# The beginning of a transformer kernel: loads on two queues, item 0 and x in three pieces, squares and a weight split shared out

## What is computed

```python
def _rmsnorm(x, g):
    r = lax.rsqrt(jnp.mean(x * x, axis=-1, keepdims=True) + EPS)
    return x * r * g

def _swiglu(x, w_gate, w_up, w_down):            # 1024 -> 2816 -> 1024
    return (silu(x @ w_gate) * (x @ w_up)) @ w_down

# ffn1:  x + 0.5 * rmsnorm(_swiglu(_rmsnorm(x, pre_g), ...), post_g)
```

## Time and profile before

| | |
|---|---|
| median of three runs | 1083.72 us |
| the profiled execution | 1082.73 us |
| its span, first to last instruction | 1080.9 us |
| TensorE matmuls, busy | 1065.5 us (99%) |
| VectorE busy | 794.4 us (73%) |
| ScalarE busy | 592.9 us (55%) |
| GpSimd busy | 218.5 us (20%) |
| moved by DMA | 189.64 MB |

### The profile page before, as it was taken

One profiled execution on the slowest core, in us unless ns is written; L12 is line 12 of the kernel. 1 busy time (PEld: TensorE's weight loads), 2 busy tenths in 40 slices (PEclk: granted clock), 3 DMA queues, 4 the chain that ended last, 5 costly groups with the idle time before them and its releaser, 6 DMA issues.

```text
span 1080.9 us, 18754 instructions
## 1 busy us (share of the span) xinstructions
PE 1065.5 (99%) x7012; PEld 937.8 (87%) x7012; DVE 794.4 (73%) x1096; ACT 592.9 (55%) x857; POOL 218.5 (20%) x225
## 2 busy tenths in 40 slices
PE   9999999999999999999999999999999999999997
PEld 8888889888788888898997988888899888888886
DVE  5867776897678888766795788777559557777674
ACT  6546544767766445455796644544433565544453
POOL 0006000031069997000000497000000000000001
PEclk9999999999999999999999999999999999999999
DMA  7765455342445556552434655645434235545541
GB/s 260 294 246 200 182 177 199 132 154 79 145 167 186 216 179 229 181 208 98 142 134 157 251 190 178 233 175 181 169 133 161 97 121 188 221 175 184 207 152 39
DMA packets 37025, 189.64 MB, mean 175 GB/s; under 512 B 3824, under 2 KB 4592, under 8 KB 22640
## 3 DMA queue, kind: packets, MB, share of 16 engines
q1 hardware_dynamic: 34528, 181.22, 46.5%
q10 hardware_dynamic: 2160, 6.70, 1.8%
q0 software_dynamic: 288, 1.05, 0.3%
HBM read 187.90 MB, written 1.05 MB: 175 GB/s over the span
## 4 chain that ended last, share of the span: by engine, by line
PE 88%; DVE 6%; ACT 4%; issue 1%; DMA 1%; SPq 0%; DVEq 0%; ACTq 0%
PE ps L567 23%; PE ps L638 19%; PE ps L572 12%; PE ps L679 7%; PE ps L803 6%; PE ps L579 6%; PE ps L599 2%; DVE gu_low L1833 1%; PE ps L701 1%; PE ps L527 1%; PE ps L614 1%; PE ps L755 1%; PE ps L626 1%; PE ps L786 1%; PE ps L768 1%
## 5 line engine op out<-in xcount | busy, mean ns | idle before, releaser
L567 PE MATMUL ps<-hT,gu_high 128*128 128x512 f32 x1152 | 286.7, 391 | 0.0
L567 PEld LDWEIGHTS ps<-hT,gu_high 128*128 128x128 f32 x1152 | 211.5, 188 | 41.5 <-DVE gu_low L1968 0.4
L1968 DVE TENSOR_TENSOR gu_low<-gu_raw,gu_high 128x2048 fp32r<-128x2048 f32 x83 | 196.3, 2366 | 7.6 <-ACT gu_high L1307 4.6
L572 PEld LDWEIGHTS ps<-hT,gu_low 128*128 128x128 f32 x1152 | 157.2, 190 | 11.2
L1307 ACT ACTIVATE gu_high<-gu_raw 128x2048 fp32r<-128x2048 f32 x84 | 160.4, 1909 | 9.3 <-PE ps L579 8.2
L572 PE MATMUL ps<-hT,gu_low 128*128 128x256 f32 x1152 | 160.6, 282 | 0.0
L1283 ACT ACTIVATE ffn_s<-ffn_s 128x256 f32<-128x256 f32 x88 | 36.8, 418 | 181.3 <-DVE ffn_s L1935 145.4
L1972 DVE TENSOR_TENSOR dn_low<-dn_raw,dn_high 128x1024 fp32r<-128x1024 f32 x84 | 112.2, 1336 | 2.7 <-ACT dn_high L1315 2.7
L1950 DVE TENSOR_TENSOR ffn_s<-ps,ffn_s 128x256 f32<-128x256 f32 x72 | 30.6, 425 | 108.4 <-ACT ffn_s L1295 108.4
L1315 ACT ACTIVATE dn_high<-dn_raw 128x1024 fp32r<-128x1024 f32 x84 | 88.7, 1056 | 35.6 <-PE ps L638 35.6
L1182 ACT ACTIVATE gu_high<-gu_raw 128x2048 fp32r<-128x2048 f32 x37 | 70.8, 1914 | 67.5 <-PE ps L679 36.6
(11 more groups left out here) (337 smaller groups left out, 1874.3 us busy)
## 6 DMA issues: line engine op xcount, KB each, us to landing
gu_raw<-in_wgu SPq DMA_DIRECT2D x126, 1024.0 KB, 4.8
dn_raw<-in_wdn SPq DMA_DIRECT2D x88, 512.0 KB, 5.4
x<-in_x SPq DMA_DIRECT2D x2, 512.0 KB, 5.4
gu_raw<-in_wgu SPq DMA_DIRECT2D x2, 512.0 KB, 6.5
scratch<-in_glu ACTq DMA_DIRECT2D x1, 1024.0 KB, 7.5
scratch<-in_biasM ACTq DMA_DIRECT2D x1, 1024.0 KB, 5.0
s5in<-in_s5in ACTq DMA_DIRECT2D x1, 768.0 KB, 4.4
out_x<-scratch SPq DMA_DIRECT2D x3, 256.0 KB, 2.4
```

The source lines that it names most:

```text
L567: nc.tensor.matmul(out, gu[0][:, sl, o:o + P], hT_both[:, k, :, :].rearrange("p a s -> p (a s)"), start=k == 0, stop=False)
L572: i = nc.tensor.matmul(out[:, 0:SEQ], gu[1][:, sl, o:o + P], hT[0][:, k, :], start=False, stop=k == KC - 1)
L1968: nc.vector.tensor_tensor(gu[1][:, sl, :], gu_raw[:, sl, :], gu[0][:, sl, :], ALU.subtract).then_inc(s["gu_split"], 1)
```

## The change

Loads:
- x goes to ScalarE's queue, in three pieces: columns 0 to 255, 256 to 511, 512 to 1023; `cols` is issued after the first. Item 0 stays on SyncE's queue, in three pieces of the same columns (for gate and up together). Item 1 is loaded in two halves with a semaphore each. dn 0 and dn 1 now come ahead of the loop over guarded loads.

TensorE: chunks are transposed in pairs (both tiles of chunks 2k and 2k + 1) by `first_transposes(k)`: pairs 0 and 1 before the first matmul, pair 2 before k = 2, pair 3 before k = 4. The seven fillers are gone.

ScalarE: each quarter of item 0 waits for its own piece. Then: item 1's first half, the square of tile 0, item 1's second half, both roots, dn 0.

VectorE: the square of tile 1 by a `tensor_tensor_reduce` between item 1's two remainders. dn 0's remainder moves to GpSimd, and VectorE waits for it before it adds its own first count to `dn_split`.

```diff
-            for h, arrived in enumerate(("first_loaded", "gu_loaded0")):
-                hs = slice(h * 512, h * 512 + 512)
-                sp_.dma_start(x[:, :, hs], a["x"][:, :, hs]).then_inc(s["x_loaded%d" % h], 16)
-                sp_.dma_start(by_gate(gu_raw)[:, :, hs], first_item[:, :, hs]).then_inc(s[arrived], 16)
+            for arrived, ks in (("first_loaded0", slice(0, 256)), ("first_loaded1", slice(256, 512)),
+                                ("gu_loaded0", slice(512, 1024))):
+                sp_.dma_start(by_gate(gu_raw)[:, :, ks], first_item[:, :, ks]).then_inc(s[arrived], 16)
+            for w, arrived in enumerate(("second_loaded", "gu_loaded1")):
+                ws = slice(w * 1024, w * 1024 + 1024)
+                sp_.dma_start(gu_raw[:, 1, ws], a["wgu"][1][:, ws]).then_inc(s[arrived], 16)
...
-            for g in range(1, 4):
-                if g == 2:
-                    for d in range(2):
-                        load_dn(d, d, guard=False)
-                load_gu(g, g % 2, guard=g >= 2)
+            for d in range(2):
+                load_dn(d, d, guard=False)
+            for g in range(2, 4):
+                load_gu(g, g % 2)
...
+            def first_transposes(k):
+                pe.wait_ge(s["x_loaded%d" % min(k, 2)], 16)
+                for t in range(TT):
+                    for c in range(2 * k, 2 * k + 2):
+                        i = nc.tensor.transpose(chunk(0, c)[:, t * P:(t + 1) * P], x[:, t, c * P:(c + 1) * P],
+                                                ident[:, :])
+                        if t == 1:
+                            i.then_inc(s["hT_psum"], 1)
...
-                    if k == (2 if n else 1):
+                    if n == 0 and k in (2, 4):
+                        after_two(k // 2 + 1)
+                    elif n and k == 2:
                         after_two()
...
-            for t in range(TT):
-                transposes(0, t, 0)
-            fill(7, 1)
-
-            ffn(0, 0, lambda: rest_of_x(0))
+            first_transposes(0)
+            first_transposes(1)
+
+            ffn(0, 0, first_transposes)
...
+            act.dma_start(x[:, :, 0:256], a["x"][:, :, 0:256]).then_inc(s["x_loaded0"], 16)
             act.dma_start(cols[:, :], a["cols"]).then_inc(s["early_loaded"], 16)
+            for k, ks in ((1, slice(256, 512)), (2, slice(512, 1024))):
+                act.dma_start(x[:, :, ks], a["x"][:, :, ks]).then_inc(s["x_loaded%d" % k], 16)
...
+            second_high(0, "second_loaded", "first_high")
+            for k in range(3):
+                act.wait_ge(s["x_loaded%d" % k], 16)
+            nc.scalar.activation(postw[:, 0, :], x[:, 0, :], ACT.Square,
+                                 accum_out=st["ss"][:, 0:1]).then_inc(s["sq_done"], 1)
+            second_high(1, "gu_loaded1", "gu_high")
+            act.wait_ge(s["sq_done"], TT)
+            for t in range(TT):
+                nc.scalar.activation(st["std"][:, t:t + 1], st["ss"][:, t:t + 1], ACT.Sqrt,
+                                     scale=1.0 / D, bias=col(COL_EPS)).then_inc(s["std_ready"], 1)
             dn_high_first(0)
-            norm(0)
...
+                        if static and (f, i) == (0, 0):
+                            dve.wait_ge(s["dn_split"], 1)
...
+            nc.vector.tensor_tensor_reduce(out=postw[:, 1, :], in0=x[:, 1, :], in1=x[:, 1, :], scale=1.0, scalar=0.0,
+                                           op0=ALU.mult, op1=ALU.add, accum_out=st["ss"][:, 1:2]) \
+              .then_inc(s["sq_done"], 1)
             dve.wait_ge(s["gu_high"], 2)
             gu_low_half(1, 1)
-            next_splits(0)
             norm_rows(0)
...
+            pool.wait_ge(s["dn_high"], 1)
+            nc.gpsimd.tensor_tensor(dn[1][:, 0, :], dn_raw[:, 0, :], dn[0][:, 0, :], ALU.subtract) \
+              .then_inc(s["dn_split"], 1)
```

More of the change, by code:

```diff
@@ L298, in build @@
             "tile_psum", "tile_high", "tile_low", "pair_t0", "pair_half",
-            "x_loaded0", "x_loaded1", "early_loaded", "s5c_loaded", "late_loaded", "ab_loaded", "cd_loaded",
+            "x_loaded0", "x_loaded1", "x_loaded2", "early_loaded", "s5c_loaded", "late_loaded", "ab_loaded", "cd_loaded",
             "biasM_loaded", "gu_loaded0", "gu_loaded1", "dn_loaded0", "dn_loaded1", "gpost_loaded", "gpost_ffn2", "gpost_final", "out_stored",
-            "ident_loaded", "first_loaded", "first_high", "first_low", "filler_set",
+            "ident_loaded", "first_loaded0", "first_loaded1", "second_loaded", "first_high", "first_low", "filler_set",
             "sq_done", "std_ready", "last_half", "half_high", "rinv_ready", "rB_psum", "rB_ready", "hT_psum", "hT_high", "hT_low",
@@ L517, in _ @@
         def _(pe):
+            def first_transposes(k):
[6 more added lines that the diff above has]
+                            i.then_inc(s["hT_psum"], 1)
             def transposes(n, t, h):
                 for c in range(4 * h, 4 * h + 4):
-                    if c % 4 == 0 and n == 0:
-                        pe.wait_ge(s["x_loaded%d" % h], 16)
-                    elif c % 4 == 0:
+                    if c % 4 == 0:
                         wait_x(pe, n - 1, 2 * t + h)
@@ L1213, in norm @@
                 for t in tiles:
[L1214 to L1218, removed]
+                    for half in range(2):
+                        wait_x(act, n - 1, 2 * t + half)
                     nc.scalar.activation(postw[:, t, :], x[:, t, :], ACT.Square,
@@ L1419, in _ @@
             warm_sqrt()
[L1420 to L1423, removed]
+            for k, arrived in enumerate(("first_loaded0", "first_loaded1", "gu_loaded0", "gu_loaded0")):
+                act.wait_ge(s[arrived], 16)
                 ks = slice(k * 256, k * 256 + 256)
@@ L1427, in _, with second_high @@
                 norm_out(0, range(2 * k, 2 * k + 2))
[L1428 to L1431, removed]
+            def second_high(w, arrived, done):
+                act.wait_ge(s[arrived], 16)
+                ws = slice(w * 1024, w * 1024 + 1024)
+                nc.scalar.activation(gu[0][:, 1, ws], gu_raw[:, 1, ws], ACT.Copy).then_inc(s[done], 1)
+            second_high(0, "second_loaded", "first_high")
[8 more added lines that the diff above has]
+                                     scale=1.0 / D, bias=col(COL_EPS)).then_inc(s["std_ready"], 1)
             dn_high_first(0)
-            norm(0)
             step.mark(nc.scalar.activation(st["warm"][:, 0:1], col(COL_HALFPI), ACT.Silu))
```

## The result

The changed kernel takes 1086.62 us (median of 8 runs, 1085.79 to 1088.31), the kernel before 1083.74 beside it (8 runs, 1083.36 to 1084.17): a ratio of 1.0027, interval 1.0018 to 1.0036. It is 2.9 us slower. The forecast was 1083.2, with a chance of 0.04 for slower by over 0.2%. So its trace shows less of the loss than the median holds.

The account below looks back on a forecast made before the run. TensorE, with 88% of the chain, bounds the kernel; its start waits for loads. Earlier start -0.5 and smaller pieces +0.4 put T at 10.5, gain 0.5, other parts 0: 1083.2 us from 1083.72, range 1082.1 to 1084.3.

Parts of the forecast that it names:

- T: Landing of the second half of item 0 and of x: 10.5 us forecast, 10.6 before the change.
- the rule T + 5.43: End of item 0's matmuls, where item 1's begin: 5.43 us of TensorE work after T.
- 11.0 - T: Gain at item 1's start, from 16.45 - 5.43 - T: 0.5 us forecast.
- Rival 3: TensorE's clock rises later, through gaps at the start and no fill: 2.0 us lost, 0.5 won, 1085.2; chance 0.10.
- 0 directly: Direct cost of removing fill(7, 1), 1.73 us of TensorE filler said to stand in idle time.
- The small pieces: Loads of x and item 0 in 1 KB runs delay T by 0.4 us, bounds 0 and 0.7.
- rival 1: Small pieces eat the earlier start, the slowest engine deciding: T 10.8 to 11.1, time 1083.7; chance 0.23.
- rival 2: Two queues feed the opening loads better than one: T 9.4, gain 1.6 us, time 1082.1; chance 0.17.
- The 0.5 us of earlier start: x's first piece, issued at 0.73 instead of 1.2, brings T forward by 0.5 us, bounds 0.2 and 0.8.
- The first landing: First pieces of x and item 0 land at 5.1; first matmul at 7.8 instead of 9.59; ceiling 1.8 us.
- T to the end of item 0: TensorE's transposes and matmuls after T: 0.44 + 12 x 0.12 + 0.44 + 24 x 0.12 + 0.23 = 5.43 us.
- The chores: Squares, roots and dn's remainder shared among ScalarE, VectorE and GpSimd stay hidden: cover 0.35 for rinv, 1.0 for act_low.

Follow-up runs that it names:

- both edits: The changed kernel with the seven fillers back and x's last piece on SyncE's queue ahead of item 0's last piece: 1083.78 us, ratio 0.9993.
- the queue alone: The changed kernel with x's last piece moved to SyncE's queue ahead of item 0's last piece, without fillers: 1085.79 us, ratio 1.0007.
- run 84: Not a follow-up run: a DMA run of 2 KB, which took an engine 84 ns in the median.
- the two kernels above where item 2 came late: The changed kernel with fillers back and item 1 held until x's last piece landed, 1085.19 us; or with all of x on SyncE's queue, 1084.97 us.

## Why the prediction was wrong, step by step

- **The failed step: T.** "Chunks 4 to 7 still need the second half of item 0 and of x: 2.24 MB in all, the same bytes as before", and both at 10.5. For item 0 it held (10.6). For x it was 11.97, since the 2.24 MB were not the only ones moved by then: item 1 was in the same turns, and by 12 us 1.1 MB of it and of the loads behind it had been moved. With item 1 held back, x landed at 10.5. I had ordered bytes as on one queue, and on two queues there is no common order. With 11.97 for T the rule T + 5.43 gives 17.4 for item 1's start and 11.0 - T a loss of 1.0 us, most of the 1.38 measured.
- **Rival 3 was the other half.** The mechanism was right, the place was not: the clock did not rise late, it fell again, in the gap ahead of the second pair of chunks. I had put that gap at 1.0 us (6.3 to 7.3), it was 2.42, because x's second piece landed at 8.4. "6 us of filler stay, and little is idle" was the argument against, and it rested on landings that were wrong. Its price of 2.0 us for the clock came out at 2.0 (both edits against the queue alone), partly by luck, since it was reckoned for another stretch; the 0.5 to be won did not come. Its chance of 0.10 was too low for an edit whose line I had closed with "0 directly".
- **The small pieces.** I took +0.4, at most 0.7. On one queue it was 1.0 in one order and 0.3 in another. The traces give the work itself: a 1 KB run took an engine 46 ns in the median and a 2 KB run 84, so 64 runs of 1 KB cost 0.3 us more than their bytes in 2 KB runs. The rest is when the slowest engine is through, which rival 1 named. The second pair, reckoned for 7.3, landed at 8.1 (item 0) and 8.4 (x), and at 8.2 and 7.5 with all on one queue; no run isolates why.
- **Two queues feed better (rival 2, T = 9.4)** did not happen: item 0's last piece at 10.6, x's at 11.97. The 0.5 us of earlier start was in the forecast too, and no run shows it by itself.
- **The first landing.** 5.1 was near: ScalarE began at 5.35, behind cols, which landed at 5.1, and not at 4.6. The first matmul came at 8.95, not 7.8, for the second pair's sake.
- **T to the end of item 0.** 5.43 reckoned, 5.86 measured (17.83 - 11.97): the first four transposes took 0.74 and not 0.44, and 0.11 us went to chunk 6's wait.
- **The chores held, all of them.** The rows of the changed kernel:

```profile
17.62 1.22 DVE L2145 CUSTOM_DVE_ANT_0 scratch<-x 128x1024 f32<-128x1024 f32 x1
...
18.77 0.08 DVE L2145 DVE_READ_ACCUMULATOR2_ANT small<- 128x1 f32 x1
...
20.41 2.38 POOL L2622 TENSOR_TENSOR dn_low<-dn_raw,dn_high 128x1024 fp32r<-128x1024 f32 x1 [19.96 <-ACT dn_high L1218]
...
20.73 0.60 PE L553 MATMUL ps<-ident,small 128*128 128x128 f32 x4
...
23.72 0.43 DVE L1981 TENSOR_TENSOR act_low<-ffn_s,act_high 128x256 fp32r<-128x256 f32 x1
```

VectorE's square is 1.30 us (1.3 to 1.4 reckoned), rinv's broadcast has no idle before it, GpSimd's remainder ends at T + 10.8 (T + 10.3 reckoned), and act_low behind it takes 0.43. SyncE's later issues hurt nobody here: ScalarE rounds item 2 at 22.74 without a wait. In the two kernels above where item 2 came late they did, so the cover was thin.

## What to carry to other kernels

Two queues have no common order: what is wanted next must not stand on one queue while something with longer runs and no hurry stands on the other, because the DMA engines gave both queues as many runs, of whatever length. Before fillers are taken out, look at how long TensorE will then stand still, with the landings taken late and not as hoped, and price the work behind the gap at 1.2 GHz. Where two losses end at the same moment, as here, mend them one at a time and together; mending one alone showed 0.3 to 1.4 us of the 2.6 to 3.4 (each kernel against the one before on its chip).

## What the hardware showed

- Of two queues with work, both got about as many runs: 113 and 115 (SyncE's of 2 and 4 KB, ScalarE's of 2), 199 and 183 (both of 2 KB), 125 and 113 (of 2 and 8 KB, and of 2), each from 8 to 10 us.
- A load of 512 KB with 2 KB runs landed 7.8, 8.8, 9.3 to 10.1, or 10.8 us after its issue, as no, 2, 4 or 8 KB runs stood behind the shared bytes on the other queue.
- TensorE at 2.4 GHz stood still for 2.42, 2.85, 3.07, 3.13 and 4.36 us, and each time fell to 1.2 GHz, between 0.9 us before the end of the gap and 1.1 behind it. It stayed there although dense matmuls ran again (8.8 to 12.2; 8.1 to 11.5; 14.6 to 18.0; 7.7 to 14.5; 10.9 to 14.4). With gaps of 0.93 and 1.67 us in one kernel it stayed at 1.00. In the gaps of 2.85 and 3.13 us it fell before any matmul had run again.
- The time of a kernel without fillers scatters with its clock: with x's last piece moved alone, the run with a mean clock of 0.999 took 1083.72 us, those with 0.996 and less 1085.99 to 1087.78. So the clock does not fall in every execution of such a kernel. Both edits together stay at 0.998 or more and within 1083.16 to 1085.62.
